# First block's rows from stationary one-hot matrices, one joined stage for choice and experts, second choices weighted on TensorE

## The reference, cut to what matters

```python
grp_logits = xt @ w_grp + b_grp                  # 4 groups, xt = rmsnorm(x1, g_ffn)
g_sel = argmax(grp_logits); p_g = softmax(grp_logits)[g_sel]
top_val, top_idx = top_k(e_logits of the group, 2)
weights = p_g * softmax(top_val)                 # two choices per row
# rows sorted by expert, in blocks:
h = silu(xb @ w_e1[e]) * (xb @ w_e3[e])          # 1024 -> 512
y[row] += (h @ w_e2[e]) * weight                 # 512 -> 1024
x2 = x1 + y
```

## Time and profile before

| | |
|---|---|
| median of 3 executions | 1227.87 us (1223.87 to 1229.82) |
| profiled execution: time | 1227.32 us |
| profiled execution: span | 1225.5 us |
| PE busy | 1084.5 us (88%) |
| DVE, ACT, POOL busy | 428.3, 354.5, 391.2 us |
| HBM read and written | 269.30 MB, 26.54 MB |
| mean granted clock of TensorE | 0.956 |

### The profile page before, as it was taken

How to read it: one execution, slowest core, us unless ns; L and a number is a source line. 1 busy time by engine, 2 the same in 40 slices (tenths; PEclk the granted TensorE clock), 3 DMA queues, 4 the chain that set the end, 5 groups by cost and what they waited for, 6 DMA issues and landing times. The chain is left out here.

```text
span 1225.5 us, 20512 instructions
## 1 busy us (share of the span) xinstructions
PE 1084.5 (88%) x8243; PEld 832.5 (68%) x8243; DVE 428.3 (35%) x988; ACT 354.5 (29%) x748; POOL 391.2 (32%) x428
## 2 busy tenths in 40 slices
PE   5999899899999989999999896888888888887783
PEld 4998898798999877888898673454445444444441
DVE  6698733891111363342323442211211111111116
ACT  6547633352222644453332431000000000000000
POOL 4454458841211443322554101221212112211100
PEclk9999989898988989999999887999999999999996
DMA  7332236255322531114421898999999999999997
GB/s 130 90 83 70 69 83 167 48 158 130 91 74 61 205 103 38 50 53 139 141 79 44 304 425 354 425 428 424 430 425 429 427 429 427 429 427 430 427 427 264
DMA packets 149678, 289.10 MB, mean 236 GB/s; under 512 B 43668, under 2 KB 119028, under 8 KB 132832
## 3 DMA queue, kind: packets, MB, share of 16 engines
q1 hardware_dynamic: 94224, 249.40, 52.4%
q10 hardware_dynamic: 49632, 27.46, 8.3%
q0 software_dynamic: 5744, 11.15, 2.4%
HBM read 269.30 MB, written 26.54 MB: 241 GB/s over the span
## 5 line engine op out<-in xcount | busy, mean ns | idle before, releaser
L492 PE MATMUL bank<-xhi,cv_w_hi 128*128 128x272 f32 x848 | 260.1, 307 | 9.5 <-PEq L135 3.2
L478 POOL TENSOR_TENSOR cv_w_lo<-cv_w_raw,cv_w_hi 128x1024 fp32r<-128x1024 f32 (+1 forms) x69 | 167.9, 2433 | 310.6 <-ACT cv_w_hi L471 291.8
L2559 PE MATMUL bank<-e_w,b_xT 128*64 128x256 f32 x2048 | 231.0, 383 | 24.4 <-DVE b_xT L2588 14.9
L492 PE MATMUL bank<-xhi,cv_w_lo 128*128 128x272 f32 x848 | 251.2, 296 | 0.0
L492 PE MATMUL bank<-xlo,cv_w_hi 128*128 128x272 f32 x848 | 250.4, 295 | 0.0
L2559 PEld LDWEIGHTS bank<-e_w,b_xT 128*64 128x64 f32 x2048 | 147.3, 138 | 98.0 <-DVE b_xT L2588 19.1
L492 PEld LDWEIGHTS bank<-xhi,cv_w_hi 128*128 128x128 f32 x848 | 165.8, 195 | 18.2 <-issue 10.2
L492 PEld LDWEIGHTS bank<-xlo,cv_w_hi 128*128 128x128 f32 x848 | 166.3, 196 | 0.9
L492 PEld LDWEIGHTS bank<-xhi,cv_w_lo 128*128 128x128 f32 x848 | 165.8, 196 | 0.0
L2571 PE MATMUL bank<-e_w,b_hiddenT 128*64 128x512 f32 x512 | 116.9, 598 | 18.9 <-DVE b_hiddenT L2596 18.9
L2524 POOL COPY b_target<-slot_target 128x1 int32 (+1 forms) x31 | 5.5, 178 | 309.0 <-ACT b_y L2581 288.9
(11 more groups left out here) (447 smaller groups left out, 1641.9 us busy)
## 6 DMA issues: line engine op xcount, KB each, us to landing
e_w<-in_w_e SPq DMA_DIRECT2D x96, 2048.0 KB, 32.4
cv_w_raw<-in_w_in ACTq DMA_DIRECT2D x34, 512.0 KB, 4.2
cv_w_raw<-in_w_in SPq DMA_DIRECT2D x18, 512.0 KB, 3.9
cv_w_raw<-in_w_br_b ACTq DMA_DIRECT2D x8, 512.0 KB, 4.1
o_raw<-in_w_out SPq DMA_DIRECT2D x16, 256.0 KB, 3.7
y_rows<-choice_rows SPq DMA_DIRECT2D x8, 512.0 KB, 11.7
g_values_gates<-g_z_stage ACTq DMA_DIRECT2D x12, 272.0 KB, 4.6
f_gates<-g_values_gates SPq DMA_DIRECT2D x2, 1088.0 KB, 8.7
```

Source lines behind the costliest of these rows:

```text
L478: self.k.nc.gpsimd.tensor_tensor(self.wlo[:, s, 0:nk, :], self.raw[:, s, 0:nk, :], self.whi[:, c % OPS, 0:nk, :].bitcast(F32), ALU.subtract)\
L492: last = self.k.nc.tensor.matmul(self.bank(c, h)[:, 0:HALF], w, x[:, d, cols], start=(d == 0 and n == 0), stop=(d == nk - 1 and n == 2))
L2559: last = nc.tensor.matmul(k.bank[bank][sl[a], 0:FH], xT[:, d, :], w[slot][:, d, FH * a:FH * a + FH], start=(d == 0), stop=(d == KD - 1))
```

## The change

- The two stages are one block, `choices_and_experts`: no barrier and no reset between them. The routing stage's temporaries lie in the room of w_e3's fourth slot.
- Block 0's rows: for every tile DVE makes columns (`first_oh`: is this row slot s of expert 0, times the row's 1/rms), and TensorE multiplies x itself by them (`first_rows`) into the bank TA, over five tiles; DVE copies TA to the buffer. The indexed gather of block 0, `place_first` and all `keep_busy` are gone.
- x stays in `x_rows`; its store and reload are gone. So there is room for three slots of each matrix (RING = 3), and a fourth of w_e1 and w_e3 that block 3 alone uses; the w_e2 of block 3 waits for block 0's. The row buffers are three instead of two.
- In a block, TensorE turns the next block's rows before it waits for the hidden product, and DVE scales them around the copy. silu writes into `b_hidden` itself.
- The matrices of block 31 are loaded in six halves, and its products wait for each half apart.
- At the end, for the last three tiles in the order the second choices are added by TensorE: diagonal matrices of the weights (`weigh`, made by ACT) times `y_rows`, into the same banks as block 31's part.
- Small ones: the last tile's normalized rows go to two buffers and two DMAs; the planning of the extra blocks moves from blocks 4 to 7 to blocks 4 to 6; POOL's descriptor scratch is 4096 instead of 8192 bytes.

```diff
-RING = 4
-PAIRS = 2
+RING = 3
+EARLY = 7
...
-            k.run(project_and_choose)
-            k.routing.close()
-            k.run(expert_blocks)
+            k.run(choices_and_experts)
...
+    k.w3.append(k.sb("e_w3_3", [128, KD, FE], F32, k.rings, high=True))
...
+    k.xn, k.xg = keep("xn", D), k.sb("b_rows", [128, RING, D // 2], F32, ctx)
+    k.first_oh = k.over("c_first_oh", [128, 5, SLOTS], F32, "b_rows")
...
+def load_half(k, sp, name, tile, part, e, loaded):
+
+    src = expert_matrix(k, name, e).rearrange("(p k) n -> p (k n)", p=128)
+    half = slice(2048 * part, 2048 * part + 2048)
+    sp.dma_start(tile[:].rearrange("p k n -> p (k n)")[:, half], src[:, half]).then_inc(loaded, 16)
...
-            sp.wait_ge(added1, 2)
-            sp.dma_start(k.keep_p[:, 0:2, :], k.x[:, 1:3, :]).then_inc(k.x_kept, 16)
...
-            sp.wait_ge(added1, 4)
-            sp.dma_start(k.keep_p[:, 2:4, :], k.x[:, 3:5, :]).then_inc(k.x_kept, 16)
...
-            sp.wait_ge(added1, 5)
-            sp.dma_start(k.keep_s, k.x[0:NS, 0, :]).then_inc(k.x_kept, 16)
...
+        sp.wait_ge(k.normed, 5)
+        sp.wait_ge(k.picked, 1)
+        load_weights(k, sp, "w_e3", k.w3, k.w3_loaded, 3, 3)
...
+                for h in range(2):
+                    g.dma_start(k.table[ROW0[t]:ROW0[t] + n, 512 * h:512 * h + 512], xn_s[h][0:n, :]).then_inc(k.last_tabled, 16)
+        g.wait_ge(tabled, 64)
+
...
-            keep_busy(5)
...
+        def first_rows(i):
+
+            t, n = tiles[i][1], tiles[i][3]
+            pe.wait_ge(columns, i + 1)
+            rows = k.x[0:n, t, :].rearrange("n (p k) -> n k p", k=KD)
+            for h in range(2):
+                last = nc.tensor.matmul(TA[64 * h:64 * h + 64, :], k.first_oh[0:n, t, :], rows[:, 4 * h:4 * h + 4, :],
+                                        start=(i == 0), stop=(i == 4))
+            if i == 4:
+                last.then_inc(placed, 1)
+
...
+        place(3, tiles[3][3])
+        for i in range(3):
+            first_rows(i)
+        count(4, tiles[4][3])
+        pe.wait_ge(chosen, 6)
+        nc.tensor.matmul(L[1][:, 0:NE], k.ones[:], run[:, 1, :], start=True, stop=True).then_inc(counted, 1)
+        for i in range(3, 5):
+            first_rows(i)
+        place(4, tiles[4][3])
...
+            v.wait_ge(ranked, i + 1)
+            V.tensor_scalar(scaled[0:n, :], k.oh[0:n, 0, t, 0:1], rr[0:n, t:t + 1], None, ALU.mult)
+            c(V.tensor_scalar(other[0:n, :], r1[1][0:n, 0:SLOTS], k.oh[0:n, 1, t, 0:1], rr[0:n, t:t + 1], ALU.mult, ALU.mult))
+            V.scalar_tensor_tensor(out=k.first_oh[0:n, t, :], in0=r1[0][0:n, 0:SLOTS], scalar=scaled[0:n, :], in1=other[0:n, :],
+                                   op0=ALU.mult, op1=ALU.add).then_inc(columns, 1)
+
...
+        v.wait_ge(counted, 6)
+        V.tensor_copy(k.total[:], L[1][:, 0:NE])
+        v.wait_ge(placed, 1)
+        V.tensor_copy(k.xg[:, 0, :], TA[:]).then_inc(k.joined, 1)
+        v.wait_ge(listed, 5)
+        c(V.tensor_tensor(sums, sums, S[:, 2 * NE:4 * NE], ALU.add))
+        V.scalar_tensor_tensor(out=k.idx[:, 0:NE], in0=sums[:, 0:NE], scalar=k.half[:, 0:1], in1=sums[:, NE:2 * NE],
+                               op0=ALU.add, op1=ALU.add).then_inc(k.picked, 1)
...
+        if ahead is not None:
+            turn(pe, b + 1, *ahead).then_inc(turned, 1)
...
+        nc.vector.tensor_tensor(hm[:], hm[:], k.bank[2][:, 0:FH], ALU.mult).then_inc(hidden, 1)
+        if ahead is not None:
+            columns(v, b + 1, 0)
+        v.wait_ge(hturned, b + 1)
+        wait(v, down, b)
+        nc.vector.tensor_copy(hT[:].rearrange("p c s -> p (c s)"), k.bank[3][:, 0:256]).then_inc(hcopied, 1)
+        if ahead is not None:
...
+    def places(b):
+
+        up_at = (b, 0) if b <= RING else ((b - 1) % RING, (b - 1) // RING)
+        return up_at + (b % RING, b // RING, b % RING, b // RING - (b % RING == 0))
...
+        for b in range(RING + 1, EARLY):
+            loads_up(sp, b, b - RING - 1, (b - 1) % RING)
+            loads_down(sp, b - 1, b - 1 - RING, (b - 1) % RING)
+        loads_down(sp, EARLY - 1, EARLY - 1 - RING, (EARLY - 1) % RING)
+        with sp.Fori(EARLY // RING, LAST // RING) as i:
+            for s in range(RING):
+                b = RING * i + s + 1
+                loads_up(sp, b, b - RING, s)
+                loads_down(sp, b, b - RING, (s + 1) % RING)
+        u, d2 = (NE - 2) % RING, (NE - 1) % RING
+        sp.wait_ge(first, NE - RING)
+        load_half(k, sp, "w_e1", k.w1[u], 0, NE - 1, k.w1_loaded[u])
+        load_half(k, sp, "w_e1", k.w1[u], 1, NE - 1, k.rest[0])
...
+        g.wait_ge(k.last_tabled, 32)
+        g.wait_ge(k.picked, 1)
+        g.wait_ge(k.cleared, RING - 1)
+        for b in range(1, RING):
+            g.indirect_dma_start(out=xg[:, b, :], out_offset=None, in_=k.halves,
+                                 in_offset=bass.IndirectOffsetOnAxis(ap=k.idx[:, b:b + 1], axis=0),
+                                 bounds_check=2 * NT - 1, oob_is_err=False).then_inc(gathered[b], 16)
+        g.wait_ge(targets, 1)
...
+        pe.wait_ge(k.joined, 1)
+        turn_rows(0).then_inc(turned, 1)
+        n = run_blocks(pe, products, beside)
...
+                last = nc.tensor.matmul(END[m][a][0:rows, :], last_rows[sl[a], t, 0:rows], y[sl[a], :], start=True, stop=alone)
...
+        for m, t in enumerate(ORDER[0:4]):
+            last = own(m, t, m < 2)
+            if m < 2:
+                last.then_inc(last_in, 1)
+        for m, t in enumerate(ORDER[2:], 2):
+            rows = TILES[t][1]
+            if m == 4:
+                pe.wait_ge(finished, 2)
+                own(m, t, False)
+            pe.wait_ge(k.got[2 * m + 1], 16)
+            for a in range(2):
+                last = nc.tensor.matmul(END[m][a][0:rows, :], weigh[0:rows, t, 0:rows], yrows[0:rows, t, 1, 512 * a:512 * a + 512],
+                                        start=False, stop=True)
+            last.then_inc(last_in, 1)
+
...
+                for t in ORDER[2:]:
+                    n = TILES[t][1]
+                    last = nc.scalar.activation(weigh[0:n, t, 0:n], k.ident[0:n, 0:n], ACT.Copy, scale=k.wt[0:n, t, 1:2])
+                last.then_inc(weighed, 1)
...
+        for m in range(2):
+            add_choice(m, 0, 0)
+            add_choice(m, 1, 2 * m + 1)
+        for m in range(2, 5):
+            add_choice(m, 0, 0)
...
-    nc = _bacc.Bacc("TRN2", target_bir_lowering=False, num_devices=1, dynamic_dma_scratch_size=8192)
+    nc = _bacc.Bacc("TRN2", target_bir_lowering=False, num_devices=1, dynamic_dma_scratch_size=4096)
```

More of the change, by code:

```diff
@@ L154, in build @@
             k.chain(None, which)
[L156 removed]
+        k.gathered = [k.sem(f"b_gathered{s}", k.top) for s in range(RING)]
         k.got = [k.sem(f"y_got{m}", k.top) for m in range(10)]
@@ new lines, in expert_blocks, with wait, fetch @@
+    gathered = k.gathered
+    stored = k.sem("b_stored")
+    lo, hi = slice(0, 64), slice(64, 128)
+    sl = (lo, hi)
+    S, M, X = k.bank[7], k.bank[6], (k.bank[0], k.bank[5])
+    def wait(eng, sem, value):
+        if not isinstance(value, int) or value > 0:
+            eng.wait_ge(sem, value)
+    def fetch(g, b, half, n, prev):
+        wait(g, turned, prev + 1)
+        nc.gpsimd.tensor_copy(at[:, half:half + 1], k.idx[:, bass.ds(b, 1)]).then_inc(index, 1)
+        g.wait_ge(index, b + 1 - RING)
+        nc.gpsimd.tensor_tensor(spare[:, 0:1], k.one[0:SLOTS, :], k.one[0:SLOTS, :], ALU.add)
+        g.indirect_dma_start(out=xg[:, half, :], out_offset=None, in_=k.halves,
+                             in_offset=bass.IndirectOffsetOnAxis(ap=at[:, half:half + 1], axis=0),
+                             bounds_check=2 * NT - 1, oob_is_err=False).then_inc(gathered[half], 16)
+        g.wait_ge(gathered[half], 16 * n + 16)
@@ L2584, in vector_part, with scalar_part, columns @@
+    def scalar_part(a, b, u, nu, d2, nd, half, m, own=False, ahead=None, halves=False):
+        a.wait_ge(first, b + 1)
+        wait(a, hturned, b)
+        nc.scalar.activation(hm[:], k.bank[1][:, 0:FH], ACT.Silu).then_inc(silu, 1)
+        a.wait_ge(down, b + 1)
+        wait(a, stored, 16 * b)
+        nc.scalar.activation(y[:], k.bank[4][:], ACT.Copy).then_inc(out, 1)
+    def columns(v, b, a):
+        if a == 0:
             v.wait_ge(turned, b + 1)
             wait(v, up, b)
-            for a in range(2):
-                f = slice(4 * a, 4 * a + 4)
-                nc.vector.tensor_tensor(xT[:, f], X[a][:, 0:4 * SLOTS].rearrange("p (k s) -> p k s", k=4),
-                                        k.gain[:, f].unsqueeze(2).broadcast_to([128, 4, SLOTS]), ALU.mult).then_inc(copied, 1)
@@ new lines, in columns, with vector_part @@
+        f = slice(4 * a, 4 * a + 4)
+        nc.vector.tensor_tensor(xT[:, f], X[a][:, 0:4 * SLOTS].rearrange("p (k s) -> p k s", k=4),
+                                k.gain[:, f].unsqueeze(2).broadcast_to([128, 4, SLOTS]), ALU.mult).then_inc(copied, 1)
```

(18 more changed lines are left out.)

1162 lines of the change are left out of this document (553 added, 609 removed).

## The result

| | before | after |
|---|---|---|
| median of 6 executions | 1228.11 us | 1216.76 us (1214.74 to 1219.00) |
| ratio, 95% interval | | 0.9909 [0.9889, 0.9930] |
| profiled execution: time, span | 1227.32, 1225.5 us | 1214.74, 1213.0 us |
| last store issued | 1222.21 us | 1209.83 us |

The account below looks back on a forecast made before the run. Weight transfers at 425 to 430 GB/s were taken to set the pace, not TensorE. Terms: -4.7 (restart) - 5.2 + 0.3 - 2.6 + 0.9 = -11.3 us, from 1227.32 to 1216.0; range for 8 in 10: 1211 to 1223.

Parts of the forecast that it names:

- Term 1: Restart of the weight stream at the seam, DMA side: `picked` at 741.7, w3_3 leaves 5.8 us earlier (2.5 to 6.8).
- a dip shorter than 3 us: Sign that the forecast is right: the traffic dip between the two stages is shorter than 3 us and near 741.
- Term 2: Restart at the seam, PE side: block 0 at 743.1, w1_4 at 748.4, a new hole of 1.1 us in the stream.
- E: End of the weight stream, 1194.4 before the change; predicted to move by -4.7 us (bounds -6.5 to 0).
- term 5: No reload of x behind the last weights: -5.2 us, with 0.3 us taken for a hole before the y_rows.
- Terms 3 and 4: Ring of three slots per matrix, and the last block's matrices loaded in halves: 0 us each.
- rival C: Ring runs dry from a PE block of 13.6 us; one hole in each of 28 blocks, +31 us, 1247; chance 0.05.
- Term 6: The end: DVE has two sums instead of four after the seventh y_rows, -2.6 us; waiting for TensorE, +0.9 (0 to 4.7).
- A: Strided read of x in first_rows slows PE: five pairs take 12 us, `picked` at 747; time 1222.2; chance 0.15.
- B: Cold end: PE stays at half clock through tiles 2, 3 and 0; +3.8 us, time 1219.8; chance 0.08.
- D: Restart bound by gathers waiting for the table's last rows: block 1's rows 6 us late, some 4 cost, 1220; chance 0.08.

## Why the prediction was right, by its own steps

The forecast was 1216.0 us; it is 1216.76, and the medians lie 11.35 us apart where 11.3 were summed. In the profiled executions, on which the terms can be read one by one, it is 12.6 us: the one of after is the fastest of its six, and its seam began 1.5 us early. So some of the agreement of the single terms is luck, and is called so below.

- **Term 1**, `picked` at 741.7: 741.98. Two errors cancel. A pair at full clock costs 2.00, not 0.91 us, so three pairs took 5.76 and not 4.3, and tile 4's 2.0 and not 1.2; but first_rows began at 730.46, 1.5 us earlier than 731.95, as the seam does in some executions. w3_3 left 5.4 us earlier (5.8 predicted), 3.9 without those 1.5. This issue is the change's main gain at the seam; the sign "a dip shorter than 3 us" did not come, it is 3.5 us long and only earlier.
- **Term 2**, block 0 at 743.1: 742.77. w2_3 at 757.1: 756.92. The gather was expected to be hidden by under 1 us: block 1's turning waited 0.39 us for it. w1_4 left at 748.17 (748.4). The hole of 1.1 us behind w3_3 is not seen as such: from 746 to 750 the shares are 0.96 and 1.06. From block 0's first product to the first weighted sum it is 449.8 us after and 450.3 before; less the reload's 5.2, that is 4.7 us more for the same weights, since block 0 came 9.2 us earlier and w3_3 only 5.4, and the y_rows left a hole of 0.8 (term 5). Predicted were 4.2 (8.9 for block 0, 4.7 for E) and 0.3 at the y_rows, 4.5 together.
- **Terms 3 and 4**, ring and halves at nothing: both right. The ring's condition was sized wrong: rival C put the limit at a block of 13.6 us, and the run without turning ahead, with 13.54, already lost 2.8 us, because of a pause in SP's order of issues that the prediction had not looked at.
- **Term 5**: +4.3 to +4.5 in Q when 2.10 MB are put back, against 5.2 for 2.23 MB. The hole ahead of the y_rows is 0.8 us (windows of 1 us from 1186: shares 0.83, 0.62 and 0.75), not 0.3. With both, the first sum came at 1192.57, 9.7 us earlier, where the terms give 9.6; 1.5 of the 9.7 is the early seam.
- **Term 6**, -2.6 and +0.9: T went from 19.96 to 17.26, -2.7. The +0.9 for TensorE was the wrong waiting: it was at clock 1.00 and never late. In its place DVE had 2.25 us of pauses for y_rows, of which the prediction had counted the last landing, but not that nothing could run before it. Here T gave 1 us more than was summed, most of what the sum missed: the -2.6 was right, and the +0.9 did not come. The run with all sums on DVE puts the worth of TensorE's part at 1.2 to 1.9 us, where 1.7 were summed. That run's T (19.20) is itself 0.8 us under that of before (19.96): its ten sums have one pause of 0.31 us where before has two of 0.80 together (0.35, and 0.45 in the earlier trace rows), and a sum takes 1.29 instead of 1.32 us. The two steps, 0.8 and 1.9, are the 2.7.

The rivals. *A*'s sign came (pairs above 1.2 us at clock 1.00), and its mechanism is right; its price is not: the strided read costs nearly double at full clock (2.00 against 1.08) and cost 0.7 us in three pairs that ran partly at half, 2.2 us in all; 12 us for five pairs was more than the 9.8 measured, and an early seam hid part of it. The Trainium skill (SBUF — State Buffer, "Door 1: The DMA port swizzle") says that up to 4 floats of stride are free and beyond that a penalty is paid; the runs agree on PE for a step of 8 floats, 1.85 times as long at clock 1.00; for steps of 2 to 4 no run here has a number. *B* didn't happen in after, where the clock was 1.00 while TensorE worked at the end; it did in part in the run with the additions between the sums. *C* didn't happen; without the turning ahead there is one gap of 1.8 us, not one in each block. *D* didn't: block 1's turning waited 0.39 us for its gather, not 6.

## What to carry to other kernels

When a stream of transfers bounds a kernel, price a joined stage by when the next transfer may be issued and by the bytes before the first consumer, not by the barrier's own wait: here the barrier put back cost PE 1.8 us and the stream 0.5 in the profile. A smaller ring of buffers is free only if the consumer keeps up before the queue has filled. Look for the longest pause in the order of issues (here 12 to 13 us, where four slots become three), and test the ring together with the step that shortens the block. When work is moved ahead of a seam, count from a point ahead of the moved work. And read the spread of the stage before the seam from several profiles: here it was as large as most of the steps.

## What had not been expected of the hardware

A float32 matmul of 64 output columns by 512 whose moving operand is read with a step of 8 floats: 2.00 us for a pair at a granted clock of 1.00, against 1.07 to 1.08 contiguous. At a clock of 0.50 a contiguous pair takes 1.97, so the strided read at full clock looks like a half clock in the timeline while the window says 1.00.
